# Two more chunks of every FFN stage turned on VectorE, their squares moved by ScalarE, and seams put in another order

## The reference

```python
def swiglu(x, w_gu, w_down):
    g, u = jnp.split(x @ w_gu, 2, axis=-1)
    return (jax.nn.silu(g) * u) @ w_down
...
        f = swiglu(rms_norm(x, ffn1_pre_g[l]), ffn1_w_gu[l], ffn1_w_down[l])
        x = x + 0.5 * rms_norm(f, ffn1_post_g[l])
```

## Time and profile before

| | us |
|---|---|
| median of 3 runs | 1891.96 |
| lowest and highest of them | 1891.42, 1892.94 |
| the profiled execution's own time | 1891.43 |
| its span in the trace | 1890.1 |
| TensorE busy | 1883.7 |
| VectorE busy | 1499.4 |
| ScalarE busy | 1100.2 |

### The profile page before, as it was taken

The page is one execution under the profiler, slowest core; times in us unless marked ns, Lnnn a source line. Parts: engine busy times, 40 slices in busy tenths (PEclk is TensorE's granted clock), DMA queues, the critical chain, the costliest instruction groups (busy, mean ns, idle before and its releaser), DMA issues.

```text
span 1890.1 us, 24908 instructions
## 1 busy us (share of the span) xinstructions
PE 1883.7 (100%) x9038; PEld 1578.3 (84%) x9038; DVE 1499.4 (79%) x2832; ACT 1100.2 (58%) x1828; POOL 153.0 (8%) x193
## 2 busy tenths in 40 slices
PE   9999999999999999999999999999999999999999
PEld 7888998888888898888888888888888888888887
DVE  6996787986798768898679867679867986857985
ACT  6555876555655586555655556555555555655553
POOL 1110030000000013000000014100000000500000
PEclk9999999999999999999999999999999999999999
DMA  7765535664566553666466645355655664535663
GB/s 249 241 220 180 191 132 180 218 202 160 197 229 211 171 187 122 201 204 202 160 203 215 206 141 186 113 179 201 201 170 177 217 208 145 181 115 182 204 201 109
DMA packets 97786, 350.25 MB, mean 185 GB/s; under 512 B 10880, under 2 KB 12032, under 8 KB 97408
## 3 DMA queue, kind: packets, MB, share of 16 engines
q1 hardware_dynamic: 95184, 340.13, 53.8%
q10 hardware_dynamic: 2448, 8.53, 1.2%
q0 software_dynamic: 32, 0.00, 0.0%
HBM read 347.57 MB, written 1.05 MB: 184 GB/s over the span
## 4 chain that ended last, share of the span: by engine, by line
PE 61%; DVE 2%; ACT 1%; issue 0%; DMA 0%; POOL 0%; POOLq 0%; DVEq 0%; ACTq 0%
PE ps_gu L492 12%; PE ps_gu L494 12%; PE ps_gu L493 12%; PE ps_acc L492 6%; PE ps_acc L494 6%; PE ps_acc L493 6%; DVE sb_wl L2061 1%; PE ps_gu L797 1%; PE ps_acc L512 1%; PE ps_gu L798 1%; PE ps_gu L799 1%; PE ps_gu L1164 0%; PE ps_acc L1125 0%; PE ps_tr L539 0%; PE ps_acc L1178 0%
## 5 line engine op out<-in xcount | busy, mean ns | idle before, releaser
L492 PE MATMUL ps_gu<-sb_wh,sb_xh 128*128 128x512 f32 (+2 forms) x1592 | 624.5, 392 | 0.0
L494 PE MATMUL ps_gu<-sb_wh,sb_xl 128*128 128x512 f32 (+2 forms) x1592 | 617.9, 388 | 0.0
L493 PE MATMUL ps_gu<-sb_wl,sb_xh 128*128 128x512 f32 (+2 forms) x1592 | 617.0, 388 | 0.0
L1365 ACT ACTIVATE sb_wh<-sb_raw,sb_const 128x512 fp32r<-128x512 f32 x346 | 249.0, 720 | 260.6 <-DMA sb_raw<-stream 148.9
L2061 DVE TENSOR_TENSOR sb_wl<-sb_raw,sb_wh 128x1024 fp32r<-128x1024 f32 (+2 forms) x294 | 350.3, 1221 | 41.5 <-ACT sb_wh L1369 39.0
L494 PEld LDWEIGHTS ps_gu<-sb_wh,sb_xl 128*128 128x128 f32 x1592 | 298.8, 188 | 60.9
L1369 ACT ACTIVATE sb_wh<-sb_raw 128x1024 fp32r<-128x1024 f32 (+2 forms) x294 | 300.8, 1042 | 81.4 <-PE ps_acc L494 42.7
L492 PEld LDWEIGHTS ps_gu<-sb_wh,sb_xh 128*128 128x128 f32 x1592 | 299.0, 188 | 58.8 <-issue 0.8
L493 PEld LDWEIGHTS ps_gu<-sb_wl,sb_xh 128*128 128x128 f32 x1592 | 299.2, 188 | 57.4
L2056 DVE SCALAR_TENSOR_TENSOR sb_wl<-sb_raw,sb_const,sb_wh 128x512 fp32r<-128x512 f32 x346 | 259.5, 750 | 107.0 <-ACT sb_wh L1366 105.8
L2123 DVE STREAM_TRANSPOSE sb_scratch<-sb_scratch 32x128 f32<-32x128 f32 x1024 | 310.2, 303 | 20.2 <-DVE sb_scratch L2114 0.5
(11 more groups left out here) (281 smaller groups left out, 1570.7 us busy)
## 6 DMA issues: line engine op xcount, KB each, us to landing
sb_raw<-stream SPq DMA_DIRECT2D x620, 512.0 KB, 4.3
sb_raw<-stream SPq DMA_DIRECT2D x8, 416.0 KB, 3.4
sb_raw<-stream SPq DMA_DIRECT2D x8, 390.0 KB, 3.1
sb_scratch<-stream SPq DMA_DIRECT2D x6, 512.0 KB, 8.6
sb_gpost<-post_gains ACTq DMA_DIRECT2D x6, 512.0 KB, 5.3
sb_params<-params ACTq DMA_DIRECT2D x2, 1128.5 KB, 7.4
sb_scratch<-gain_rows ACTq DMA_DIRECT2D x4, 512.0 KB, 6.4
sb_raw<-stream SPq DMA_DIRECT2D x4, 384.0 KB, 3.1
```

The source lines that it names most:

```text
L492: pe.matmul(out, xh, wh, start=start, stop=False)
L493: pe.matmul(out, xh, wl, start=False, stop=False)
L494: return pe.matmul(out, xl, wh, start=False, stop=stop)
L1365: go(m.wh[:, u % RING, 0:512], m.unit(u)[:, 0:512], ACT.Copy, scale=m.gpre[:, e, k:k + 1])
```

## The change

Chunks 0 and 9 are no longer turned by TensorE. For them (`by_scalar(j)`) one VectorE instruction turns all squares of both halves in place, from `hid` into `squares`, a buffer laid out like `hid`; then ScalarE moves the 16 blocks of squares to their final places in `hid_t` with 16 copies of 32 x 128 (`place_squares`), and `both_high` and `both_low` follow as for the other chunks. Only chunk 10 is still turned by TensorE (`turn_last`, `last_high`, `last_low` are the old functions under new names). The middle of a stage now covers chunks 1 to 9 alike, so `down` of chunk 0 for both halves comes after `gate_up` of chunk 1, and the order of weight units changes with it: units 4 and 5 of a stage are now gate/up units (with a gain), and units 8 and 9 are the two `down` units of chunk 0.

All seams now begin with the same function. The parts that matter of the diff:

```diff
-def squared(j):
-    return 0 < j < LAST - 1
+def by_scalar(j):
+    return j in (0, LAST - 1)
...
     def down(f, j, t, half):
-        if squared(j):
+        if j < LAST:
             pe.wait_ge(*s.both_low.at(squared_count(f, j)))
         else:
-            pe.wait_ge(*s.hid_low[t].at(turned_count(f, j)))
+            pe.wait_ge(*s.last_low[t].at(f + 1))
...
     def steady(f):
-        gate_up(f, 1, 0, 0)
-        gate_up(f, 1, 0, 1)
-        turn_hidden(f, 0, 1)
-        gate_up(f, 1, 0, 2)
-        gate_up(f, 1, 0, 3)
-        down(f, 0, 1, 0)
-        down(f, 0, 1, 1)
...
+        for j in range(1, LAST):
             for t in range(2):
+                units(f, j, t, 0, 4)
             for t in range(2):
                 down(f, j - 1, t, 0)
                 down(f, j - 1, t, 1)
+
+    def last_of_first(f):
+        units(f, LAST, 0, 0, 4)
+        units(f, LAST, 1, 0, 1)
         down(f, LAST - 1, 0, 0)
+        turn_last(f, 0)
         down(f, LAST - 1, 0, 1)
         down(f, LAST, 0, 0)
         down(f, LAST, 0, 1)
+        units(f, LAST, 1, 1, 4)
...
+    def place_squares(f, j):
+        act.wait_ge(*s.squared.at(squared_count(f, j)))
+        for units in range(4):
+            for tokens in range(4):
+                a = go(square(m.hid_t, units, tokens), square(m.squares, tokens, units), ACT.Copy)
+        a.then_inc(*s.placed.up())
...
     def turn_squares(f, j):
         for t in range(2):
             vec.wait_ge(*s.hid_done[t].at(11 * f + j + 1))
+        if by_scalar(j):
+            v = vec.transpose(m.squares, m.hid)
+        else:
+            for units in range(4):
+                for tokens in range(4):
+                    v = vec.transpose(square(m.hid_t, units, tokens), square(m.hid, tokens, units))
```

More of the change, by code:

```diff
@@ L244, in __init__ @@
         self.hid_done = [Signal(nc, f"hidden_done_{t}") for t in two]
-        self.turned = [Signal(nc, f"hidden_turned_{t}") for t in two]
+        self.turned = [Signal(nc, f"last_hidden_turned_{t}") for t in two]
         self.squared = Signal(nc, "hidden_squares_turned")
@@ L2427, in mix1 @@
         split(1)
+        both_low(f, LAST - 1)
         split(1)
-        hidden_low(f, LAST - 1, 1)
         hidden(f, LAST, 0)
-        hidden_low(f, LAST, 0)
-        split(1)
+        last_low(f, 0)
         split(1)
@@ L2441, in mix1 @@
         x_mean(e, 0)
+        hidden(f, LAST, 1)
         normed(e, 0, 0)
```

389 lines of the change are left out of this document (132 added, 257 removed).

## The result

The changed kernel takes 1924.6 us (median of 4 runs, 1924.2 to 1926.0) against 1891.8 for the kernel before on the same chip: a ratio of 1.0174, 95% interval 1.0156 to 1.0191. It is slower by 1.7%. The prediction was 1890.9, range 1885.0 to 1896.5: wrong in size and in sign. The profiled execution has a span of 1922.8 us, 32.7 more than before.

The account below looks back on a forecast made before the run. TensorE was taken as the bound, busy 1883.7 of 1890.1 us. Terms -7.3 - 1.0 - 0.6 + 0.5 + 7.3 = -1.1 us gave 1890.9 against the median; range 1885.0 to 1896.5.

Parts of the forecast that it names:

- the sum of -1.1: Whole kernel: all terms together make the profiled execution 1.1 us shorter, 1890.3 us; the forecast had chance 0.45.
- What TensorE is rid of: TensorE: 32 pairs of transposes in chunks 0 and 9 go, 0.23 us each, saving 7.3 us.
- The price of the copies: ScalarE's 16 copies of 32 x 128: 0.217 us each with overlap, 3.5 us; bounds 2.6 and 5.1.
- The chain of chunk 0: Stage starts: from silu of the second half to the end of the low part takes 9.95 us, against 10.9 available.
- all five stages that I counted at nothing: Starts of the stage from 1229 us, its sister at 1707 and three behind post and plain: no wait at chunk 0.
- the copies were mispriced: Sign: TensorE's waits at chunk 0 stand in all eight stages, not only those near 0, 290 and 750 us.
- The lateness of silu: Stages from 0, 290 and 752 us: silu of the second half starts 3.3 to 3.6 us late, 0.3 less in stage 0.
- The sum of chunk 0: Stage starts: `down` of chunk 0 waits 2.5, 2.4 and 2.4 us in three stages, 7.3 us together.
- copies that cost more: Rival, chance 0.20: copies cost more than their size, chain longer; 1896 us, or 1906 with 5.1 us and a 1.21 transpose.
- What the seams' new order does: Seams: 1.0 us less over two to mix1, 0.6 less over two to post, 0.5 more over two to mix2.
- `last_low` at mix2: Seams to mix2: TensorE waits 1.3 us for the last turned half's low part, 0.25 more in each of 2.
- What chunk 9 costs: Chunk 9: low part ready about 10.9 us after `gate_up`, `down` at 12.3 us, so covered by 1.4 us.

Follow-up runs that it names:

- run 8: Changed kernel with chunk 0's ScalarE copies in another of eight forms (partitions, block width, group) in each stage, hidden values misplaced; 1910.6 us, ran once.
- Run 2: Changed kernel with silu of chunk 0's second half, its hidden values and the turn two units earlier at every stage start, the copies one; 1911.9 us.
- Run 3: Changed kernel with 15, 17 and 14 extra matmuls filling TensorE's waits at chunk 0 in the stages from 0, 290 and 763 us; 1921.5 us.
- run 4: Changed kernel with pieces of work reordered at the seams mix1, post, mix2 and plain, nothing added; 1919.8 us.
- run 7: Changed kernel with VectorE's sixteen transposes for chunk 0, copies kept at chunk 9 alone; 1906.1 us, against 1904.5 with copies at neither.

## Why the prediction was wrong

The measured execution is 33.9 us above the sum of -1.1. By size, the waits at chunk 0 are 10.4 of it (17.7 us between starts against 7.3), the slow matmuls behind waits about 7, and the seams themselves the largest part, about 16. The terms in turn:

**What TensorE is rid of: right.** 32 transposes of hidden values are left of 96, and in stretches where only a turn of chunk 9 went, the step is -0.26 to -0.28 us, against 0.23.

**The price of the copies: the step that failed first.** "0.217 each, 3.5 us for 16". Measured 0.319, 5.10 us: the upper bound of the text. The overlap of 0.1 us that I took off stands in no row of the text for a copy of this kind. It is there for copies of 128 partitions (run 8: 0.200 apart, 0.293 long), not for these. The Trainium skill ("ScalarE: Activation LUTs", What ACT_TABLE_LOAD costs) gives an overlap of 93 ns between copies in a row; the copies of 128 partitions agree; the 16 of 32 partitions, no two of which in a row keep both groups, do not. There was a nearer row in the profile of before than the one I used: VectorE's transposes have this very pattern of squares, a length of 0.303, and 16 of them took 5.05 us, no overlap either. I read that row for another purpose.

**The chain of chunk 0.** Predicted 9.95 us, measured 11.3 to 11.85; 1.6 of it are the copies. The parts before and behind them were right to 0.3. (Behind post and plain the turn starts 2.6 us after silu and not 2.0: VectorE's unit ahead of it waits for ScalarE's part, which comes only after that silu.) With 9.95 all five stages that I counted at nothing would have waited for nothing; with 11.3 they wait 1.2 each, 6.2 us together. The text had this as the sign that "the copies were mispriced", and gave the case a chance of 0.20.

**The lateness of silu: right.** Predicted 3.4, 3.3 and 3.3 in the stages from 290, 752 and 0; measured 3.9, 3.0 and 3.0. Run 2 removes it, and with it what these three waits had above the others.

**The sum of chunk 0.** 16.4 us against 7.3. Even the rival "copies that cost more", with 5.1 us and a transpose of 1.21 besides, gave 1906, since it took the seams as forecast and the clock as full.

**The clock: not in the text.** 30 matmuls at 427 ns, 6.0 us, and 0.9 on narrower ones, behind waits of 2.75 us and more. I priced a wait at its length. Run 3 showed the extra.

**What the seams' new order does: wrong, and the largest term.** Predicted -1.1, with the pairs there -4.4; the stretches of the table moved by +17.1, of which 3.7 are the short waits at chunk 0 and 1.5 the slow matmuls behind the wait at 674 us. Right was one wait: `last_low` at mix2, 1.3 us predicted and 1.3 measured, twice. Not seen were the low half of a unit at mix1 (2.6 us on the list, twice), where two units of ScalarE stand behind squares of an x that is not ready:

```profile
197.66 1.06 ACT L1273 ACTIVATE sb_wh<-sb_raw 128x1024 fp32r<-128x1024 f32 x1
201.79 0.63 ACT L1295 ACTIVATE sb_scratch<-sb_x 128x512 f32<-128x512 f32 x1 [3.07 <-DVE sb_x L1989]
...
203.09 1.99 ACT L1273 ACTIVATE sb_wh<-sb_raw 128x1024 fp32r<-128x1024 f32 x2
```

ScalarE idles 3.07 us there in front of a square while TensorE needs the unit behind it. Also not seen: pieces of x at post and mix2 (4.5 us) and the update at plain (1.3). I had followed the chains that the old order made critical, and not each wait in the new lists with what is queued behind it. That run 4 got back only 4.8 us of this says that part of it was cover for chunk 0.

**What chunk 9 costs: nearly right.** Covered, but for 0.17 us ahead of its products in eight stages; run 7 puts it at 1.1 to 1.6 us in all.

What stays open: why behind waits of nearly the same length the clock falls in some cases and not in others, and how the +2.2 at each seam to mix2 in the table splits beyond the two waits of 1.3 and 1.5 us there, from which the wait of before has to be taken off.
